# Expert weights in whole-matrix transfers, and the down-projection of small blocks on two halves of the array

## The reference

```
h = silu(xb @ w1[e]) * (xb @ w3[e])      # w1, w3: 1024 x 512
y = h @ w2[e]                            # w2: 512 x 1024
out[token] += gate * y
```

## Time and profile before

| | |
|---|---|
| median of 3 runs | 1024.66 us (1024.5 to 1025.6) |
| the profiled execution | 1025.62 us, of which the span is 1024.0 us |
| TensorE busy | 921.0 us (90%) |
| VectorE, ScalarE, GpSimd busy | 247.6, 111.0, 157.4 us |
| read from HBM, written | 234.55 MB, 24.60 MB |
| mean granted TensorE clock | 0.957 |

### The profile page before, as it was taken

The page is one execution under the profiler, slowest core; times in us unless marked ns, Lnnn a source line. Parts: engine busy times, 40 slices in busy tenths (PEclk is TensorE's granted clock), DMA queues, the critical chain, the costliest instruction groups (busy, mean ns, idle before and its releaser), DMA issues. The chain is left out here.

```text
span 1024.0 us, 24939 instructions
## 1 busy us (share of the span) xinstructions
PE 921.0 (90%) x10522; PEld 587.5 (57%) x10522; DVE 247.6 (24%) x760; ACT 111.0 (11%) x172; POOL 157.4 (15%) x239
## 2 busy tenths in 40 slices
PE   5999999999999973999999999989988999898940
PEld 2545545455455542876777677657556685674620
DVE  1434452454534553410000000000000000000006
ACT  0211110111101110001010101010010010010004
POOL 1000000000000002112222222212112122112110
PEclk9999999999999995999999999999989999998985
DMA  8760010100101063999999999999999999999938
GB/s 340 277 251 21 22 41 0 41 21 21 41 0 43 39 247 98 394 366 390 363 387 363 370 367 369 368 372 376 368 390 375 379 384 380 355 389 363 326 70 322
DMA packets 57935, 258.22 MB, mean 252 GB/s; under 512 B 11410, under 2 KB 12490, under 8 KB 40853
## 3 DMA queue, kind: packets, MB, share of 16 engines
q1 hardware_dynamic: 47740, 238.54, 60.6%
q0 software_dynamic: 10144, 18.95, 8.1%
HBM read 234.55 MB, written 24.60 MB: 253 GB/s over the span
## 5 line engine op out<-in xcount | busy, mean ns | idle before, releaser
L1186 PEld LDWEIGHTS ps<-hT,big 128*64 128x64 f32 x8192 | 286.4, 138 | 40.1 <-issue 28.6
L1186 PE MATMUL ps<-hT,big 128*64 128x64 f32 (+8 forms) x8192 | 294.7, 233 | 14.7 <-DMA big<-in_exp_w 7.9
L1202 PE MATMUL ps<-big,poolT 128*64 128x512 f32 (+8 forms) x512 | 233.8, 609 | 11.3 <-DMA big<-in_exp_w 7.5
L1083 PE MATMUL ps<-big,hT 128*128 128x512 f32 x384 | 169.9, 602 | 3.3 <-DMA big<-in_w_in 1.9
L1202 PEld LDWEIGHTS ps<-big,poolT 128*64 128x64 f32 (+8 forms) x512 | 75.1, 152 | 145.8 <-issue 135.2
L985 DVE TENSOR_TENSOR poolT<-u,ps 128x256 f32<-128x256 f32 (+8 forms) x32 | 15.1, 472 | 505.1 <-PE ps L1186 467.4
L1083 PEld LDWEIGHTS ps<-big,hT 128*128 128x128 f32 x384 | 73.2, 193 | 94.6 <-issue 88.5
L545 POOL DMA_INDIRECT x_rows<-xn,sidx x32 | 49.4, 1545 | 385.3 <-ACT xn L695 363.3
L695 ACT ACTIVATE xn<-ps,gslot 64x1024 f32<-64x1024 f32 (+8 forms) x32 | 35.5, 1110 | 456.0 <-PE ps L1202 240.8
L525 POOL DMA_INDIRECT slot_table<-ids,dest x18 | 18.7, 1038 | 328.2 <-DVE dest L807 271.9
L1140 PE MATMUL ps<-big,yT 128*128 128x512 f32 x128 | 56.4, 593 | 0.9 <-DVE yT L874 0.9
(11 more groups left out here) (168 smaller groups left out, 469.1 us busy)
## 6 DMA issues: line engine op xcount, KB each, us to landing
big<-in_exp_w SPq DMA_DIRECT2D x192, 1024.0 KB, 25.9
big<-in_w_in SPq DMA_DIRECT2D x4, 1536.0 KB, 13.5
big<-in_w_out SPq DMA_DIRECT2D x2, 2048.0 KB, 14.9
x_rows<-xres SPq DMA_DIRECT2D x8, 512.0 KB
h_rows<-xn SPq DMA_DIRECT2D x8, 512.0 KB, 2.7
big<-x_rows SPq DMA_DIRECT2D x8, 512.0 KB, 7.3
out_y_prompt<-big SPq DMA_DIRECT2D x8, 512.0 KB, 2.9
xres<-in_x_prompt SPq DMA_DIRECT2D x1, 3072.0 KB, 11.1
```

Of the source, the lines that this page charges most:

```text
L1083: last = pe.matmul(ps[0:m, bank, :], hT[:, k, 0:m], win[:, k, part * AW:(part + 1) * AW], start=(k == 0), stop=(k == KD - 1))
L1186: last = pe.matmul(out[c * w:(c + 1) * w, j, 0:m], up_weights(n)[:, k, j * P + c * w:j * P + (c + 1) * w], xT[:, 4 * half + k, 0:m], start ...
L1202: last = pe.matmul(ps[0:m, 5 + cols, :], hhT[:, 2 * half + k, 0:m], down_weights(n)[:, k, cols * 512:(cols + 1) * 512], start=(half + k == ...
```

## The change: whole matrices, other row ownership, two array halves

1. `CH` = 3 and `CHW` = 4,096: one transfer per matrix, 2 MiB, 16 KB contiguous per partition. 6 slots instead of 12. 32 x 3 transfers instead of 32 x 6; 92 instead of 184 from the second batch on.
2. `w2` now lies with rows 4p to 4p+3 in partition p. So that `hhT` fits, the up-projection takes output column 4q + j (q = 0 to 127) for block j instead of j*128 + q: its stationary operand is read with a step of 4 floats (16 bytes) in `big`, where it was contiguous.
3. Blocks of m <= 64 put bank 5 on array columns 0 to 63 and bank 6 on columns 64 to 127 (PSUM partitions 64 to 64 + m). ScalarE then scales only the first 512 columns and VectorE the other 512 (a new instruction, and a new semaphore `y_half_ready` that GpSimd waits for ahead of the scatter).
4. `CLASSES` has four ranges instead of five. The small block has at most 64 rows for h = 1 to 10 (before: 1 to 9) and 76 rows for h = 11 to 15.

```diff
-CLASSES = ((1, 4, (96, 56)), (4, 7, (88, 64)), (7, 10, (84, 64)), (10, 13, (80, 68)), (13, 16, (76, 72)))
+CLASSES = ((1, 4, (96, 56)), (4, 7, (88, 64)), (7, 11, (84, 64)), (11, 16, (80, 76)))
 SMALL = max(c[1] for _, _, c in CLASSES)
-CH = 6
-CHW = 2048
+CH = 3
+CHW = 4096
...
             def chunk_src(e, c):
-                half = c % 2
-                if c < 4:
-                    w = (exp_w1, exp_w3)[c // 2]
-                    return w[0, e].rearrange("(p k) n -> p (k n)", k=KD)[:, half * CHW:(half + 1) * CHW]
-                return exp_w2[0, e, half * 2 * P:(half + 1) * 2 * P, :].rearrange("(k p) n -> p k n", p=P)
+                if c < 2:
+                    return (exp_w1, exp_w3)[c][0, e].rearrange("(p k) n -> p (k n)", k=KD)
+                return exp_w2[0, e].rearrange("(p k) n -> p (k n)", k=KF)
...
@@ GpSimd
+                    if in_halves(m):
+                        pool.wait_ge(y_half_ready, h)
                     pool.wait_ge(y_ready, count)
...
@@ ScalarE
-                    act.wait_ge(used, CH * b + 2)
+                    act.wait_ge(used, CH * b + 1)
...
+                    if in_halves(m):
+                        act.activation(ys[s][0:m, 0:512], ps[0:m, 5, :], ACT.Copy,
+                                       scale=gslot[s][0:m, 0:1]).then_inc(y_ready, 1)
+                        continue
...
@@ VectorE, behind the product and take_xgT
+                    if in_halves(m):
+                        dve.wait_ge(rows_out[s], 16 * h)
+                        dve.wait_ge(gate_in[s], 16 * h + 16)
+                        dve.wait_ge(used, CH * b + CH)
+                        dve.tensor_tensor(ys[s][0:m, 512:D], ps[NS:NS + m, 6, :],
+                                          gslot[s][0:m, 0:1].to_broadcast([m, 512]), ALU.mult).then_inc(y_half_ready, 1)
...
@@ TensorE
+            def up_columns(n, k, j, first):
+
+                return up_weights(n)[:, k, :].rearrange("p (q j) -> p j q", j=KF)[:, j, first:first + P // SPLIT]
...
+                        n = CH * s + part
+                        pe.wait_ge(chunk_in[n], 16 * h + 16)
+                        for k in range(KD):
+                            for j in range(KF):
+                                for c in range(SPLIT):
+                                    w = P // SPLIT
+                                    last = pe.matmul(out[c * w:(c + 1) * w, j, 0:m],
+                                                     up_columns(n, k, j, c * w),
+                                                     xT[:, k, 0:m], start=(k + j == 0),
+                                                     stop=(k == KD - 1), skip_group_check=True)
+                        last.then_inc(used, 1)
...
+                    n = CH * s + 2
+                    pe.wait_ge(chunk_in[n], 16 * h + 16)
+                    for k in range(KF):
+                        for cols in range(2):
+                            first = NS * cols if in_halves(m) else 0
+                            last = pe.matmul(ps[first:first + m, 5 + cols, :], hhT[:, k, 0:m],
+                                             down_weights(n)[:, k, cols * 512:(cols + 1) * 512],
+                                             start=(k == 0), stop=(k == KF - 1), skip_group_check=True)
+                    last.then_inc(used, 1)
```

More of the change, by code:

```diff
@@ L406, in _ @@
             sp.dma_start(x3_rows[T:T + P, :], xg[1][:, :]).then_inc(trash_zeroed, 16)
-            for n in range(10, 2 * CH):
-                sp.dma_start(chunk_dst(n, n - CH), chunk_src(FIRST + 1, n - CH)).then_inc(chunk_in[n], 16)
+            for n in range(2 * CH - 1, 2 * CH):
+                sp.dma_start(chunk[n], chunk_src(FIRST + 1, n - CH)).then_inc(chunk_in[n], 16)
             def store_h2(i, m=P):
@@ L431, in _ @@
             for n in range(CH):
-                sp.dma_start(chunk_dst(n, n), chunk_src(FIRST, n)).then_inc(chunk_in[n], 16)
+                sp.dma_start(chunk[n], chunk_src(FIRST, n)).then_inc(chunk_in[n], 16)
             store_h2(LAST, NS)
@@ L437, in load_chunk @@
             def load_chunk(e, n):
-                sp.dma_start(chunk_dst(n, n % CH), chunk_src(e, n % CH)).then_inc(chunk_in[n], 16)
+                sp.dma_start(chunk[n], chunk_src(e, n % CH)).then_inc(chunk_in[n], 16)
             def load_weights(h):
@@ L459, in _ @@
             sp.wait_ge(out_b, NT)
-            for n in range(CH, 10):
+            for n in range(CH, 2 * CH - 1):
                 load_chunk(FIRST + 1, n)
@@ L473, in _ @@
                     for c in range(CH):
-                        sp.dma_start(chunk_dst(c, c), chunk_src(e, c)).then_inc(ov_w, 16)
+                        sp.dma_start(chunk[c], chunk_src(e, c)).then_inc(ov_w, 16)
             for s in range(2):
@@ L983, in block_pair @@
                     dve.wait_ge(silu_done, b + 1)
-                    dve.wait_ge(used, CH * b + 4)
+                    dve.wait_ge(used, CH * b + 2)
                     dve.tensor_tensor(hhT[:, :, 0:m], s1T[:, :, 0:m], up3[:, :, 0:m], ALU.mult).then_inc(hhT_ready, 1)
@@ L1196, in block_pair @@
                     pe.wait_ge(hhT_ready, b + 1)
-                    for half in range(2):
-                        n = CH * s + 4 + half
-                        pe.wait_ge(chunk_in[n], 16 * h + 16)
-                        for k in range(2):
-                            for cols in range(2):
-                                last = pe.matmul(ps[0:m, 5 + cols, :], hhT[:, 2 * half + k, 0:m],
-                                                 down_weights(n)[:, k, cols * 512:(cols + 1) * 512],
-                                                 start=(half + k == 0), stop=(half + k == 2))
-                        last.then_inc(used, 1)
+                    n = CH * s + 2
[7 more added lines that the diff above has]
+                    last.then_inc(used, 1)
             pe.wait_ge(onehot_ready, 1)
@@ L1229, in _ @@
                     for k in range(KF):
[L1230 removed]
+                        last = pe.transpose(ps[:, 4, k * P:(k + 1) * P],
+                                            hh[:, :].rearrange("t (q k) -> t k q", k=KF)[:, k, :], ident[:, :])
                     last.then_inc(ov_hT, 1)
```

10 lines of the change are left out of this document (5 added, 5 removed).

## The result

| | before | after |
|---|---|---|
| median of 4 runs | 1025.1 us (1024.5 to 1027.4) | 1165.8 us (1163.9 to 1167.0) |
| ratio | | 1.137 [1.134, 1.139] |
| span of the profiled execution | 1024.0 us | 1163.8 us |
| TensorE busy | 921.0 us (90%) | 1084.3 us (93%) |
| mean granted clock | 0.957 | 0.972 |

The forecast was 1014 us in a range of 995 to 1034; the time is outside, on the other side, and within 1 us of the upper end of rival B, 1166 us. Where the runs of a kernel spread wider than 1.5%, only those within 1.5% of its fastest count in this document, which concerns step8_by16 alone (7 of its 12 runs).

What follows compares the result with a forecast made beforehand. The prediction took the transfers (573.4 us) as the bound, TensorE's savings hidden behind them. From 1025.6 us it summed -14 (rows), +2 (slots) and +1 (row counts) to 1014.6, less 1.0 to 1014 us; range 995 to 1034.

Steps and rivals of the forecast that it cites:

- rival B: Up-projection: strided loads on both halves no longer overlap, making TensorE the bound; upper end 1166 us; chance 0.16.
- What bounds: Expert blocks: weight and row transfers bound the kernel for 573.4 us, with TensorE's work just a little less.
- The step of 16 bytes: Up-projection weight loads: 9% slower, hidden, 0 in the sum; upper end 15.4 us per up-projection.
- The step of 32 bytes costs nothing: Argument against TensorE becoming the bound: the transposes' lone loads at this step run as fast as contiguous ones.
- Larger rows: Weight transfers in 16 KB rows run 3.0% faster over 459 us: -14 us, between 0 and -27.
- Coarser slots: Six whole-matrix weight slots instead of twelve are freed later, felt at the first blocks: +2 us, between 0 and 7.
- Row counts: Scatters of the expert blocks: 40 more rows in all, +1 us; 4.6 us more of TensorE, hidden.
- Two halves: Down-projections of ten small blocks save 3.5 us each, 35 us of TensorE, but 0 in the sum.
- the cover: Transfers hide TensorE's 35 us saving in small down-projections; without that cover it would be worth up to 35 us.
- Rival A: Weight transfers: row length is worth nothing, so 1028 us (1023 to 1032); chance 0.19.
- Rival C: Weight transfers: large rows pay more among the row traffic than alone, 985 to 1003 us, likeliest 998; chance 0.13.
- Rival D: TensorE: halves don't overlap (excluded), or longer waits lower the clock, 45 us; no own chance, in the forecast's upper edge.

Runs made afterwards that it cites:

- step8_by16: The changed kernel with weights read at a step of 8 bytes, `w2` in rows of 8 KB and row counts in multiples of 16: 1018.1 us, ratio 0.996.
- coarse_halves_by16: contig_rows4k with row counts in multiples of 16: 1025.3 us, ratio 1.002 to the kernel before.
- before_76: The kernel before with one number changed, the second block of h = 13 to 15 having 76 rows instead of 72: 1063.1 us, ratio 1.039.
- contig_rows4k: The changed kernel with contiguous weight loads and `w2` in one 2 MiB transfer with rows of 4 KB: 1069.0 us, ratio 1.042 to the kernel before.
- before_step16: The kernel before with only the 16-byte step and `w2` in rows of 8 KB: 1194.1 us, ratio 1.164.
- coarse_no_halves: contig_rows4k with the old row counts and without the halves: 1052.7 us, ratio 1.028 to the kernel before.
- one_stream_step16: The changed kernel with one up-projection load of 128 columns in place of two of 64, still at the 16-byte step: 1674.3 us in one run.

## Why the prediction was wrong

- **What bounds** was right: the transfers, with TensorE close behind. That closeness (551 us of work beside 573 of transfers) was said, and rival B even named the 52 us from which TensorE decides; the forecast gave it too little weight.
- **"The step of 16 bytes ... I take the 9%: hidden, 0"** is the step that failed. It measured 15.5 to 15.6 us per up-projection, which is the upper end; nothing between the ends occurred. The error was to price two loads that overlap by one load that runs alone. The lone stream in the earlier trace rows pays 9% because it is already at 0.113 us per 128 columns; two overlapping halves need the same columns in 0.060. A rate that one stream just reaches can't be had twice. "The step of 32 bytes costs nothing", counted against rival B, was the same mistake: on two halves it costs as much as 16 bytes.
- **Rival B** had mechanism, place and size right (1166 us by its sum, 1165.8 measured) at a chance of 0.16. That it met the time within 1 us is luck: its 714 us contain the last down-projection and the 573 they are set against do not, so that its own numbers give 134 us more, 1159, and not 141. Measured were 136 us more in the expert blocks and 4 behind them. And its "no longer overlap" is shown as half the pace, with the two loads still side by side. It was the only unknown whose upper end exceeded everything else in the sum, some five times over (152 us beside 27 for the rows), and the only row for its lower end came from another arrangement. The range left it out.
- **Larger rows, -14 us**: wrong in sign. Without the step, and with row counts that spare the gathers, large transfers with long rows cost some 7 us (coarse_halves_by16), and 14 us with `w2` included. The 430 and 446 GB/s of the earlier trace rows are short stretches without gathers; in the mix of the stage the gain is 381 against 378. The sign in GB/s was right, and I had left out the small transfers between the long packets, whose landing came 3 us later.
- **Coarser slots, +2 us**: right in size (1019.4 against 1017.8 us, not to be told from 0).
- **Row counts, +1 us**: wrong by far. I counted rows and not how a number of rows is spread: 72 to 76 costs 39 us in before_76. In the changed kernel it is hidden, since there TensorE is the bound, but for the last scatter, which no TensorE work covers (4 us); with the step removed it appears as 44 us (contig_rows4k against coarse_halves_by16).
- **Two halves, 0**: right, as the cover said. Right too was that they count once the cover is gone: 28 us between before_step16 and the changed kernel, with the row counts in it.
- **Rival A** (1028 us) lies near coarse_halves_by16 (1025 us) only by chance, since that has other row counts; with the old ones it is 1053 us (coarse_no_halves). **Rival C**: the runs speak against it, since the kernels with 16 KB rows for `w1` and `w3` and for all three matrices ended later, not sooner, than the one with 8 and 4 KB. **Rival D**: the granted clock was 1.00 in the changed kernel's expert blocks, where TensorE hardly waits; it was 0.92 over contig_rows4k, where it waits. Its 45 us are called "just within" a slack of 41 and are above it.

So the +141 us are one cost that shows, the step, with some 4 us of the last scatter, and two that hide behind it, row counts and large transfers.

## What to carry to other kernels

An operation that runs twice side by side must be priced as a pair: a small penalty of a lone stream can be the end of the overlap. Before an access pattern is changed for the sake of a DMA, count how often the busiest engine then comes to a new 16-byte line. And a table of row counts that feeds gathers and scatters should be tried in steps of 16 before anything else is tuned: it was worth more here (8 us gained, or 39 lost) than transfers of twice the size, which gained nothing.

## What the runs showed of the hardware that I had not expected

- Weight loads of 64 columns on the two halves of the array's columns keep their full pace only as long as each finds its next column in the same 16-byte line: 0.058 us per pair contiguous, 0.060 at a step of 8 bytes, 0.120 at 16 and at 32. The Trainium skill ("SBUF — State Buffer", Door 1: The DMA port swizzle) states that a line of 16 bytes must be hit at least twice for the full rate. On two halves the runs agree with this: 8 bytes give two hits per line and cost nothing much, 16 bytes give one and double the time. The figure that the same passage draws from it, 4 floats as the step that is free, they don't bear out: 4 floats are the 16 bytes of the change. For the lone streams of the earlier trace rows the same rule has a price of 9% at most.
- A last scatter of 76 rows held GpSimd for 11.4 us, one of 72 for 6.1, one of 80 for 6.0, with 3.8, 11.5 and 13.1 rows in flight.
- Beside 2 MiB transfers with rows of 16 KB for `w1` and `w3`, the gate gathers land 3 us later (7.6 to 10.8 us) at the same 378 GB/s.
- In one_stream_step16 the granted clock was 0.61 with TensorE without a pause, which I can't explain from the runs.
